# A decoder trunk's feed-forwards as one stream of seven-product blocks, with the down projection and with GpSimd making sums

## The chip, the cores and the metric

The kernel runs on one core of a Trainium2 chip. The metric is the device time of one launch in microseconds. The core's engines are named as in the profile: PE (matrix products), DVE (VectorE), ACT (ScalarE), POOL (GpSimd) and SP (SyncE, which issues the DMAs). They run side by side, each through its own instructions in their order, and wait for one another by semaphores.

## The reference

Two decoder layers run over 520 tokens: 512 of a new sequence and 8 single ones that continue older sequences. Each layer is a feed-forward, a mixer (latent attention in the first, a short convolution in the second) and another feed-forward. Cut to what matters here:

```python
D_MODEL = 1024
D_FF = 2816

def rmsnorm(x, g):
    xf = x.astype(jnp.float32)
    inv = lax.rsqrt(jnp.mean(xf * xf, axis=-1, keepdims=True) + EPS)
    return (xf * inv).astype(x.dtype) * g

def swiglu(h, wg, wu, wd):
    return (jax.nn.silu(h @ wg) * (h @ wu)) @ wd

    for i in range(DEPTH):
        xp = xp + 0.5 * swiglu(rmsnorm(xp, norm_ffn1[i]), w_ffn1_gate[i], w_ffn1_up[i], w_ffn1_down[i])
        ...
        xp = xp + mp
        xs = xs + ms
        xp = xp + 0.5 * swiglu(rmsnorm(xp, norm_ffn2[i]), w_ffn2_gate[i], w_ffn2_up[i], w_ffn2_down[i])
```

All is float32, and there are four feed-forwards, each with 1024 x 2816 weights for gate and up and 2816 x 1024 for down.

## The kernel before

The residual stream `xT` lies transposed in SBUF: 8 tiles of 128 features by 520 tokens, the tokens in two halves of 260. Every product of two float32 matrices is made of three matmuls: ACT rounds an operand to the "hi" part, DVE subtracts it from the operand and gets the "lo" part, and PE adds hi x hi, hi x lo and lo x hi in PSUM. So every weight passes through ACT (`split_hi`, `first_hi`, `up_hi`, ...) and DVE (`split_lo`, `first_lo`, ...), and so does every activation.

A feed-forward has 22 tiles of 128 hidden features, in two chunks of 11 (`CHUNK`). A tile needs the gate and the up product of all 8 feature tiles. The string `KINDS` says how: "C" is a plain tile (`plain_tile`, 2 x 8 x 3 matmuls for each half of the tokens, 96), "S" a block of seven products in place of eight (`block_tile`), in the manner of Strassen and Winograd: gate and up are the two columns, the two halves of the features the inner dimension, the two halves of the tokens the rows. Each product is `half_product` with 4 x 3 matmuls, 84 in all. Four of the seven use sums of weights, which POOL makes in `weight_sums` (four instructions of 512 elements a tile), and sums of token halves, which DVE and ACT make once for a feed-forward (`mix_diff`, `mix_base`, `mix_sums`, `mix_round`, `mix_rest`). Of the 22 tiles 13 are blocks; the first tile of each chunk is plain too and comes through `split_hi` and `split_lo`. The seven products of a block go into seven PSUM banks; DVE adds them up afterwards (`gate_first`, `gate_second`, `up_base`, `up_both`), multiplies by `inv` (the token's norm), ACT takes the silu, and DVE makes `hid_t`, which is rounded into `g_hi` and `g_lo`.

The split parts of the weights lie in a ring of six halves (`RING`), four in `w_hi`/`w_lo` and two in `x_hi`/`x_lo`; a part may be split as soon as PE has used the part six before it (`part_used`). The down projection of a chunk is plain: 8 output tiles x 11 x 3 x 2 = 528 matmuls, from units that go through `w_hi` alone; DVE scales each output tile and adds it to `xT`. In the second chunk's down projection the next stage's normalised input is made tile by tile (`publish_act`, `publish_dve`). SP loads each weight tile (512 KB) into one of the four slots of `raw` when the slot is free. PE does nothing but matmuls; its order is that of the code: two units, the tiles of the chunk, the down projection. At a stage's start `norm_pe` sums the squares, and `norm_dve` and `norm_act` make `inv`, with a reciprocal on DVE.

## Time and profile before

| | |
|---|---|
| median of three runs | 2437.41 us (2435.6 to 2437.86) |
| span of the profiled execution | 2426.2 us |
| PE busy | 2371.8 us, 98% |
| DVE busy | 1543.2 us, 64% |
| ACT busy | 987.8 us, 41% |
| POOL busy | 344.5 us, 14% |

The profile is one execution. Its span goes from the first to the last instruction on the core; the time of a run is some 11 us longer than that. Busy time counts an engine's instructions from start to end, overlapping ones once. Matmuls are pipelined: one of 260 columns has a duration of some 283 ns, but starts follow one another faster, so that a stretch is best read by its number of matmuls and its length. "PEclk" is the clock granted to PE, as a share of the full 2.4 GHz.

### The profile page before, as it was taken

To read this page: it belongs to the slowest core of one execution; us is meant where nothing else is said; L and a number is where in the kernel's file an instruction comes from. 1 tells how busy PE (TensorE), PEld (TensorE's weight loads), DVE (VectorE), ACT (ScalarE), POOL (GpSimd) and SP (SyncE) were. 2 spreads that over 40 slices of the span, in tenths; PEclk is the share of its full clock that TensorE was granted. 3 is DMA by queue.
4 is the path that set the end of the run, shared out by engine and by line. 5 is a ranking of instruction groups with operands and counts; after the bars stand their busy time and mean duration, and the time that the engine had idled before them with its cause. 6 is when DMAs were issued, how large, how long until landed. Compare 5 with 4: busy or idle time off the path is not lost.

```text
span 2426.2 us, 47136 instructions
## 1 busy us (share of the span) xinstructions
PE 2371.8 (98%) x18561; PEld 2307.0 (95%) x18561; DVE 1543.2 (64%) x2361; ACT 987.8 (41%) x1926; POOL 344.5 (14%) x226
## 2 busy tenths in 40 slices
PE   7999999999999999999999999999999999999998
PEld 7999999875999999989999999999999999999998
DVE  7855865555555555547865767864765666874773
ACT  5422433464455555534432434432433224432431
POOL 1412410000000000000312410312310000331320
PEclk9999999999999999999999999999999999999999
DMA  4324324210211111203323323323333332323332
GB/s 125 104 82 118 88 85 126 90 37 26 62 34 50 47 46 44 62 10 87 97 89 111 94 84 102 96 83 109 98 88 104 88 90 87 94 85 115 89 88 79
DMA packets 373257, 199.76 MB, mean 82 GB/s; under 512 B 31680, under 2 KB 369686, under 8 KB 373064
## 3 DMA queue, kind: packets, MB, share of 16 engines
q1 hardware_dynamic: 372884, 197.03, 28.1%
q8 instruction: 126, 2.06, 0.4%
q14 instruction: 67, 0.55, 0.1%
q10 hardware_dynamic: 180, 0.11, 0.0%
HBM read 194.27 MB, written 2.87 MB: 81 GB/s over the span
## 4 chain that ended last, share of the span: by engine, by line
PE 89%; DVE 6%; issue 2%; ACT 2%; DMA 0%; SPq 0%; ACTq 0%; DVEq 0%; POOL 0%; POOLq 0%
PE ps L1960 16%; PE ps L412 15%; PE ps L416 14%; PE ps L414 14%; PE ps L733 7%; PE ps L734 7%; PE ps L735 7%; PE ps L1886 1%; PE ps L1749 1%; PE ps L1774 1%; PE ps L1898 1%; ACT sq L2244 1%; PE ps L1889 1%; PE ps L1773 1%; DVE mix_lo L680 0%
## 5 line engine op out<-in xcount | busy, mean ns | idle before, releaser
L401 DVE TENSOR_TENSOR w_lo<-raw,w_hi 128x512 fp32r<-128x512 f32 (+2 forms) x200 | 202.9, 1014 | 346.1 <-ACT w_hi L395 341.0
L395 ACT CAST w_hi<-raw 128x512 fp32r<-128x512 f32 (+2 forms) x200 | 174.0, 870 | 466.7 <-PE ps L416 413.1
L412 PE MATMUL ps<-g_hi,w_hi 128*128 128x260 f32 x1408 | 284.5, 284 | 0.3
L416 PE MATMUL ps<-g_hi,w_lo 128*128 128x260 f32 x1408 | 283.7, 283 | 0.0
L414 PE MATMUL ps<-g_lo,w_hi 128*128 128x260 f32 x1408 | 283.4, 283 | 0.0
L629 POOL TENSOR_TENSOR wsum<-raw 128x512 f32<-128x512 f32 x52 | 73.4, 1411 | 1206.2 <-DMA raw<-in_w_ffn_up 869.3
L412 PE MATMUL ps<-h_hi,w_hi 128*128 128x260 f32 x1168 | 236.9, 284 | 5.1 <-DVE h_lo L2596 2.2
L416 PE MATMUL ps<-h_hi,w_lo 128*128 128x260 f32 x1168 | 235.5, 283 | 0.0
L414 PE MATMUL ps<-h_lo,w_hi 128*128 128x260 f32 x1168 | 235.4, 283 | 0.0
L2007 ACT ACTIVATE ksq<-ps 128x384 f32<-128x384 f32 (+1 forms) x384 | 146.8, 456 | 196.6 <-PE ps L1960 196.6
L412 PEld LDWEIGHTS ps<-g_hi,w_hi 128*128 128x128 f32 x1408 | 216.9, 188 | 1.1 <-issue 1.1
L414 PEld LDWEIGHTS ps<-g_lo,w_hi 128*128 128x128 f32 x1408 | 217.5, 188 | 0.0
L416 PEld LDWEIGHTS ps<-g_hi,w_lo 128*128 128x128 f32 x1408 | 217.2, 188 | 0.0
L412 PEld LDWEIGHTS ps<-h_hi,w_hi 128*128 128x128 f32 x1168 | 180.4, 189 | 6.3 <-DVE h_lo L2596 2.4
L416 PEld LDWEIGHTS ps<-h_hi,w_lo 128*128 128x128 f32 x1168 | 180.7, 189 | 0.0
L414 PEld LDWEIGHTS ps<-h_lo,w_hi 128*128 128x128 f32 x1168 | 180.5, 189 | 0.0
L1960 PE MATMUL ps<-wuk_hi,latT_hi 128*128 128x384 f32 (+2 forms) x768 | 173.7, 334 | 6.3 <-DVE latT_lo L2078 2.9
L1960 PE MATMUL ps<-wuk_lo,latT_hi 128*128 128x384 f32 (+1 forms) x768 | 173.5, 334 | 0.0
L1960 PE MATMUL ps<-wuk_hi,latT_lo 128*128 128x384 f32 (+1 forms) x768 | 162.2, 319 | 0.0
L882 ACT ACTIVATE silu_t<-gate_t 128x520 f32<-128x520 f32 x88 | 56.4, 641 | 254.5 <-DVE gate_t L1041 164.9
L2086 DVE TENSOR_REDUCE kss<-ksq 128x8 f32<-128x1024 f32 x128 | 154.7, 1209 | 0.0
L733 PE MATMUL ps<-mix_hi,w_hi 128*128 128x260 f32 x520 | 148.3, 285 | 0.8 <-DVE w_lo L606 0.8
(416 smaller groups left out, 5989.1 us busy)
## 6 DMA issues: line engine op xcount, KB each, us to landing
raw<-in_w_ffn_gate SPq DMA_DIRECT2D x88, 512.0 KB, 3.9
raw<-in_w_ffn_up SPq DMA_DIRECT2D x88, 512.0 KB, 4.4
raw<-in_w_ffn_down SPq DMA_DIRECT2D x64, 448.0 KB, 3.8
raw<-in_w_ffn_down SPq DMA_DIRECT2D x64, 256.0 KB, 2.7
cache<-in_cache_latent SPq DMA_DIRECT2D x128, 128.0 KB, 2.0
raw<-in_w_conv_in SPq DMA_DIRECT2D x24, 512.0 KB, 3.8
raw<-in_w_o_attn SPq DMA_DIRECT2D x8, 512.0 KB, 4.2
cache<-in_cache_krope SPq DMA_DIRECT2D x128, 32.0 KB, 1.8
```

Of the source, the lines that this page charges most:

```text
L395: nc.scalar.copy(w_hi[:, un.half, 0:n] if dst is None else dst, src).then_inc(unit_hi_made, 1)
L401: nc.vector.tensor_tensor(w_lo[:, un.half, 0:n], src, w_hi[:, un.half, 0:n], ALU.subtract).then_inc(unit_lo_made, 1)
L412: nc.tensor.matmul(o[b], hi, mh[:, x0 + b * HALF:x0 + (b + 1) * HALF], start=start, stop=False)
L414: nc.tensor.matmul(o[b], hi, ml[:, x0 + b * HALF:x0 + (b + 1) * HALF], start=False, stop=False)
L416: mm = nc.tensor.matmul(o[b], lo, mh[:, x0 + b * HALF:x0 + (b + 1) * HALF], start=False, stop=stop)
L629: nc.gpsimd.tensor_tensor(wsum5[:, 0, :], u1, u2, ALU.add).then_inc(sums_made, 1)
L733: nc.tensor.matmul(o, hi[:, kc], mh(k), start=k == 0, stop=False)
L734: nc.tensor.matmul(o, hi[:, kc], ml(k), start=False, stop=False)
L735: mm = nc.tensor.matmul(o, lo[:, kc], mh(k), start=False, stop=k == KH - 1)
L1960: mm = nc.tensor.matmul(ps[:, o + e, 0:nn], x, wd[:, c, c0:c0 + nn], start=(c == 0 and q == 0), stop=(c == KC - 1 and q == 2))
L2007: ins = nc.scalar.activation(ksq[:, t % 2, c0:c0 + nn], ps[:, o + e, 0:nn], ACT.Square)
L2086: nc.vector.tensor_reduce(kss[:, s, t, :], ksq[:, t % 2, :].rearrange("p (h d) -> p h d", h=H), AX.X, ALU.add).then_inc(kss_made, 1)
```

## The change

A feed-forward has no chunks any more. Its work is a list `ORDER` of 34 entries: the first tile (T), two plain ones (C), then 19 gate-and-up blocks (S) and 12 blocks of the down projection (D), which stand in three groups of four between the S. A D block takes two output tiles as the two columns, a group's pairs of hidden tiles (4, 4 and 3 pairs, `PAIRS`) as the inner dimension, and the token halves as the rows: seven products of 12 (or 9) matmuls. All blocks, S and D, share one code on each engine (`block`). So 31 blocks follow one another, each with four weight sums on POOL. The order of the seven products is new: m1, m2, m6, m3, m7, m5, m4, and three of them go on in the bank of m1, so that PSUM adds them; ACT copies the bank out in between (`keep_first`, `keep_second`, `keep_third`), and PE waits for the copy (`kept`) before it goes on in it.

For the down blocks the hidden tiles are needed as seven pieces of 260 columns: three raw and four sums. After each odd tile POOL makes the sums of the pair (`pair_mix`, one instruction of 520 elements and two of 260), ACT rounds all seven pieces (`pair_hi`, 1820 elements) and DVE subtracts (`pair_lo`, 1820). For the last pair, which the next block needs at once, both go in two parts. At the start of a feed-forward the normalised input gets the same seven pieces, for each of four pairs of feature tiles: DVE scales by gain and `inv` (`scaled_dve`), POOL mixes (`mix_pool`), ACT and DVE split (`set_hi`, `set_lo`). POOL also adds the down blocks' results to `xT` (`first_add`, `second_add`) and squares to `acc` for the next norm (`square_add`). The blocks' results need no product with `inv`. The core of the diff, its new side (the PE, ACT and DVE versions of `block` in this order; that of ACT ends with `silu` for an S block):

```diff
+        ORDER = ([("T", 0, 0), ("C", 0, 1), ("C", 0, 2)] + [("S", 0, y) for y in range(3, 8)] + [("S", 1, 0)]
+                 + [("D", 0, y) for y in range(4)] + [("S", 1, y) for y in range(1, 8)] + [("S", 2, 0)]
+                 + [("D", 1, y) for y in range(4)] + [("S", 2, y) for y in range(1, 6)] + [("D", 2, y) for y in range(4)])
+        SIZE = {"T": 0, "C": 6, "S": 8, "D": 8}
+        GATE, UP = 0, 2
+        M12, M63, M75, M4 = 0, 2, 4, 6
+        RING = 6
...
+        def weight_sums(pool, bk):
+            u1, u2, g1, g2 = bk.raw_half(1, 0), bk.raw_half(1, 1), bk.raw_half(0, 0), bk.raw_half(0, 1)
+            w = bk.width
+            s6, s3, s7, s5 = wsum63[:, 0:w], wsum63[:, w:2 * w], wsum75[:, 0:w], wsum75[:, w:2 * w]
+            ahead = blocks[bk.at][bk.b - 1] if bk.b > 3 else blocks[bk.at - 1][-1] if bk.at else None
             for j in (1, 0):
...
+                bk.loaded(pool, j)
             if ahead:
...
+                pool.wait_ge(part_lo_made, ahead.end(M75, 2))
+            nc.gpsimd.tensor_tensor(s5, u1, u2, ALU.add).then_inc(sums_made, 1)
+            pool.wait_ge(sums_made, 4 * bk.s + 1)
+            nc.gpsimd.tensor_tensor(s6, s5, g1, ALU.add).then_inc(sums_made, 1)
+            pool.wait_ge(sums_made, 4 * bk.s + 2)
+            nc.gpsimd.tensor_tensor(s3, s6, g2, ALU.add).then_inc(sums_made, 1)
+            nc.gpsimd.tensor_tensor(s7, u2, s6, ALU.subtract).then_inc(sums_made, 1)
...
+        def scaled_dve(dve, at, k):
+            bk = blocks[at][0]
+            f = scaled(at)[:, k % 2]
             if k >= 2:
...
+                dve.wait_ge(set_made, own_sets(at, k - 1))
+            for o, y in ((EA, k), (OA, k + KH)):
+                g = KD * GAIN[bk.stage] + y
+                ins = nc.vector.scalar_tensor_tensor(out=f[:, o * HALF:(o + 2) * HALF], in0=xT[:, y * T:(y + 1) * T],
+                                                     scalar=gain[:, g:g + 1], in1=inv[:], op0=ALU.mult, op1=ALU.mult)
+            ins.then_inc(scaled_made, 1)
...
+        def first_mix(tensor_tensor, f):
+            ea = f[:, EA * HALF:EB * HALF].unsqueeze(1).to_broadcast([P, 2, HALF])
+            return tensor_tensor(two(f[:, M0 * HALF:M1 * HALF]), ea, two(f[:, EB * HALF:OB * HALF]), ALU.subtract)
...
+        def pair_mix(pool, bk):
+            pool.wait_ge(hid_made, bk.t + 1)
+            pairs_read(pool, bk)
+            first_mix(nc.gpsimd.tensor_tensor, mixes[:]).then_inc(pair_mixed, 1)
+            pool.wait_ge(pair_mixed, 3 * bk.pair + 1)
+            nc.gpsimd.tensor_tensor(piece(M1), piece(M0), piece(OA), ALU.subtract).then_inc(pair_mixed, 1)
+            pool.wait_ge(pair_mixed, 3 * bk.pair + 2)
+            nc.gpsimd.tensor_tensor(piece(M3), piece(M1), piece(OB), ALU.add).then_inc(pair_mixed, 1)
...
+            nc.scalar.copy(pair_at(bk.at, bk.pair)[0][:, c0:c1], mixes[:, HALF + c0:HALF + c1]).then_inc(set_hi_made, n)
...
+            nc.vector.tensor_tensor(lo[:, c0:c1], mixes[:, HALF + c0:HALF + c1], hi[:, c0:c1], ALU.subtract).then_inc(set_made, n)
...
+                nc.gpsimd.tensor_tensor(xT[:, x0:x0 + T], xT[:, x0:x0 + T], gate_t[:], ALU.add).then_inc(first_added, 1)
...
+            for bk in blocks[at][3:]:
+                old = blocks[at][bk.b - 1]
+                if old.kind == "S" and old.odd:
+                    pair_mix(pool, old)
+                if bk.b + 1 < BLOCKS:
+                    weight_sums(pool, blocks[at][bk.b + 1])
+                elif more:
+                    for k in range(2, 6):
+                        square_add(pool, nc.gpsimd.tensor_tensor, n + 1, k)
+                if bk.out:
+                    first_add(bk)
+                    if bk.c < 2:
+                        second_add(bk)
+                    elif more and bk.d in (1, 2):
+                        square_add(pool, nc.gpsimd.tensor_tensor, n + 1, bk.d - 1)
...
+            def block(bk):
+                pe.wait_ge(part_lo_made, bk.end(M12, 2))
+                banks_free(bk)
+                rest, late = range(bk.pairs), range(0)
+                if bk.last_pair:
+                    rest, late = range(bk.pairs - 1, bk.pairs), range(bk.pairs - 1)
+                    pe.wait_ge(set_made, pair_sets(at, PAIRS_ALL * (at + 1) - 1))
+                    half_product(bk, M12, A, EB, True, False, late)
+                    half_product(bk, M12 + 1, B, OB, True, False, late)
+                    pe.wait_ge(part_lo_made, bk.end(M63, 2))
+                    half_product(bk, M63 + 1, C, OA, True, False, late)
+                    pe.wait_ge(set_made, pair_sets(at, PAIRS_ALL * (at + 1)) - 1)
+                elif bk.out and bk.d == 0:
+                    pe.wait_ge(set_made, pair_sets(at, PAIRS_ALL * at + sum(PAIRS[:bk.c + 1])))
+                half_product(bk, M12, A, EB, not late, True, rest).then_inc(part_used, 1)
+                half_product(bk, M12 + 1, B, OB, not late, True, rest).then_inc(part_used, 1)
+                pe.wait_ge(part_lo_made, bk.end(M63, 2))
+                pe.wait_ge(kept, 3 * bk.s + 1)
+                if bk.last_pair:
+                    half_product(bk, M63, A, M1, False, False, late)
+                    pe.wait_ge(set_made, pair_sets(at, PAIRS_ALL * (at + 1)))
+                half_product(bk, M63, A, M1, False, True, rest).then_inc(part_used, 1)
+                half_product(bk, M63 + 1, C, OA, not late, True, rest).then_inc(part_used, 1)
+                pe.wait_ge(part_lo_made, bk.end(M75, 2))
+                pe.wait_ge(kept, 3 * bk.s + 2)
+                half_product(bk, M75, A, M2, False, True).then_inc(part_used, 1)
+                half_product(bk, M75 + 1, E, M0, True, True).then_inc(part_used, 1)
+                pe.wait_ge(part_lo_made, bk.done)
+                pe.wait_ge(kept, 3 * bk.s + 3)
+                half_product(bk, M4, A, M3, False, True).then_inc(part_used, 2)
...
+            def keep_second(bk):
+                act.wait_ge(part_used, bk.end(M63))
+                nc.scalar.copy(gate_t[:, 0:HALF], ps[:, bk.bank, 0:HALF]).then_inc(kept, 1)
...
+            def block(bk):
+                old, nxt = own[bk.b - 1], own[bk.b + 1] if bk.b + 1 < BLOCKS else None
+                shown = more and bk.out and bk.c == 2 and bk.d > 0
+                k = 2 * bk.d - 2 if bk.out else 0
+                if bk.last_pair:
+                    pair_hi(act, old, RAW_PART)
+                m75_hi(act, bk)
+                if bk.last_pair:
+                    pair_hi(act, old, MIX_PART)
+                keep_first(bk)
+                m4_hi(act, bk)
+                if old.kind == "S" and old.odd and not bk.last_pair:
+                    pair_hi(act, old)
+                if shown:
+                    publish_hi(act, n + 1, k)
+                keep_second(bk)
+                if shown:
+                    square_act(act, n + 1, k)
+                if nxt:
+                    first_hi(act, nxt)
                 else:
...
+                    next_unit(0)
+                keep_third(bk)
+                if shown:
+                    publish_hi(act, n + 1, k + 1)
+                if nxt:
+                    m63_hi(act, nxt)
                 else:
...
+            def block(bk):
+                old, nxt = own[bk.b - 1], own[bk.b + 1] if bk.b + 1 < BLOCKS else None
+                shown = more and bk.out and bk.c == 2 and bk.d > 0
+                k = 2 * bk.d - 2 if bk.out else 0
+                pair = old.kind == "S" and old.odd
+                after(old)
+                if bk.last_pair:
+                    pair_lo(dve, old, RAW_PART)
+                    pair_lo(dve, old, MIX_PART)
+                m75_lo(dve, bk)
+                second_made(bk)
+                m4_lo(dve, bk)
+                if pair and not bk.last_pair:
+                    pair_lo(dve, old)
+                if shown:
+                    publish_lo(dve, n + 1, k)
+                first_begun(bk)
+                if nxt:
+                    first_lo(dve, nxt)
+                elif Unit(u0 + 2).n < LAST_UNIT:
+                    split_lo(dve, Unit(u0 + 2))
+                first_made(bk)
+                up_made(bk)
+                if nxt:
+                    m63_lo(dve, nxt)
+                elif Unit(u0 + 3).n < LAST_UNIT:
+                    split_lo(dve, Unit(u0 + 3))
+                if shown:
+                    publish_lo(dve, n + 1, k + 1)
```

What that makes of the orders, at three places. First POOL in the first feed-forward. Before, its last preparation and its first sums (`wsum5` and `wsum63` are the weight sums, `raw` the loaded weights):

```order
L2514 AFFINE_SELECT own<-own 8x64
L629 TENSOR_TENSOR wsum5<-raw 128x512
L633 TENSOR_TENSOR wsum63<-wsum5,raw 128x512
L635 TENSOR_TENSOR wsum63<-wsum63,raw 128x512
L638 TENSOR_TENSOR wsum5<-raw 128x512
```

After, in the block that follows an odd tile (`mixes` holds the pair's pieces, `wsum75` and `wsum63` the weight sums of the next block):

```order
L728 TENSOR_TENSOR mixes<-mixes 128x520
L772 TENSOR_TENSOR mixes<-mixes 128x260
L774 TENSOR_TENSOR mixes<-mixes 128x260
L705 TENSOR_TENSOR wsum75<-raw 128x512
L707 TENSOR_TENSOR wsum63<-wsum75,raw 128x512
L709 TENSOR_TENSOR wsum63<-wsum63,raw 128x512
L710 TENSOR_TENSOR wsum75<-raw,wsum63 128x512
```

Ahead of the four sums of the next block now stand the three sums of the pair, and they wait for the odd tile's `hid`.

Second, ACT around a block in the first feed-forward, before (L593, L602 and L612 are the block's weight sums, L564 and L574 the next tile's weights, L891 the copy of m1's bank, L882 silu, L886 the rounding of `hid_t`):

```order
L593 CAST w_hi<-wsum5 128x512
L602 CAST w_hi<-wsum63 128x1024
L886 CAST g_hi<-hid_t 128x520
L891 COPY up_t<-ps 128x260
L612 CAST x_hi<-wsum5 128x512
L564 CAST w_hi<-raw 128x1024
L574 CAST w_hi<-raw 128x1024
L882 ACTIVATE silu_t<-gate_t 128x520
```

After, from the m7 and m5 weight sums of the block that follows an odd tile (L677) to the next block's m6 and m3 (L667), and its silu:

```order
L677 CAST w_hi<-wsum75 128x1024
L999 COPY gate_t<-ps 128x260
L688 ACTIVATE x_hi<-raw 128x512
L782 CAST pairs1<-mixes 128x1820
L1003 COPY gate_t<-ps 128x260
L647 CAST w_hi<-raw 128x1024
L1016 COPY mixes<-ps 128x260
L667 CAST w_hi<-wsum63 128x1024
L990 ACTIVATE sq<-gate_t 128x520
```

The rounding of the pair's 1820 elements stands between the first and the second copy of the bank.

Third, DVE at the start of the first feed-forward, from the reciprocal, before:

```order
L470 RECIPROCAL sq<-inv 128x520
L997 TENSOR_TENSOR gate_t<-ps,inv 128x520
L668 TENSOR_TENSOR mix_f<-mix_f 128x260
L669 SCALAR_TENSOR_TENSOR mix_f<-xT,gain,mix_f 128x260
L671 SCALAR_TENSOR_TENSOR mix_f<-xT,gain,mix_f 128x260
L1013 TENSOR_TENSOR hid_t<-ps,silu_t 128x520
L668 TENSOR_TENSOR mix_f<-mix_f 128x260
L669 SCALAR_TENSOR_TENSOR mix_f<-xT,gain,mix_f 128x260
L671 SCALAR_TENSOR_TENSOR mix_f<-xT,gain,mix_f 128x260
L1017 TENSOR_TENSOR g_lo<-hid_t,g_hi 128x520
L680 TENSOR_TENSOR mix_lo<-mix_f,mix_hi 128x4x260
```

After (`scaled2` is the scaled input, `hs` its split pieces):

```order
L604 RECIPROCAL sq<-inv 128x520
L1100 TENSOR_TENSOR gate_t<-ps,inv 128x520
L721 SCALAR_TENSOR_TENSOR scaled2<-xT,gain,inv 128x520 x2
L1109 SCALAR_TENSOR_TENSOR mixes<-ps,inv 128x520
L1113 TENSOR_TENSOR mixes<-mixes,sq 128x520
L721 SCALAR_TENSOR_TENSOR scaled2<-xT,gain,inv 128x520 x2
L1100 TENSOR_TENSOR gate_t<-ps,inv 128x520
L651 TENSOR_TENSOR x_lo<-raw,x_hi 128x1024
L747 TENSOR_TENSOR hs<-scaled2,hs 128x1820
L721 SCALAR_TENSOR_TENSOR scaled2<-xT,gain,inv 128x520 x2
L747 TENSOR_TENSOR hs<-scaled2,hs 128x1820
L721 SCALAR_TENSOR_TENSOR scaled2<-xT,gain,inv 128x520 x2
```

Where single sums of 260 elements were made on DVE, there are now scalings of 520 (two at a time) and low parts of 1820, and the sums between them are POOL's.

## Rows read from the trace of the kernel before

**Rows 1.** The page, part 1 (PE) and part 4 (engines).

```profile
PE 2371.8 (98%) x18561; PEld 2307.0 (95%) x18561; DVE 1543.2 (64%) x2361; ACT 987.8 (41%) x1926; POOL 344.5 (14%) x226
...
PE 89%; DVE 6%; issue 2%; ACT 2%; DMA 0%; SPq 0%; ACTq 0%; DVEq 0%; POOL 0%; POOLq 0%
```

**Rows 2.** Busy time by stretch; the four stretches are the four feed-forwards.

```profile
core 0: us, PE busy (x) PEld busy (x) DVE busy (x) ACT busy (x) POOL busy (x), PEclk, DMA share, GB/s
12.00:389.20 377.20, 369.33 (x3033) 367.84 (x3034) 262.12 (x346) 147.87 (x218) 83.80 (x52) 0.99 0.34 96
1122.80:1488.50 365.70, 364.38 (x3020) 363.03 (x3019) 255.61 (x329) 140.16 (x203) 85.20 (x52) 1.00 0.33 94
1488.50:1854.20 365.70, 363.99 (x3018) 362.68 (x3017) 255.47 (x330) 140.08 (x203) 85.21 (x52) 1.00 0.33 96
2042.30:2413.70 371.40, 367.10 (x3028) 365.92 (x3027) 245.53 (x316) 130.46 (x188) 85.74 (x52) 0.99 0.30 87
```

**Rows 3.** The same view of one down projection of 528 matmuls.

```profile
145.20:208.80 63.60, 63.57 (x528) 63.57 (x529) 26.74 (x35) 14.00 (x18) 1.62 (x2) 1.00 0.37 106
```

**Rows 4.** The timeline, DVE and POOL: start us, us, engine, line, operation.

```profile
280.89 1.23 DVE L568 TENSOR_TENSOR w_lo<-raw,w_hi 128x1024 fp32r<-128x1024 f32 x1 [0.68 <-ACT w_hi L564]
281.10 2.18 POOL L635 TENSOR_TENSOR wsum<-wsum,raw 128x512 f32<-128x512 f32 x1
283.23 1.31 POOL L638 TENSOR_TENSOR wsum<-raw 128x512 f32<-128x512 f32 x1
283.48 1.61 DVE L1041 TENSOR_TENSOR gate_t<-gate_t,inv 128x520 f32<-128x520 f32 x1
```

**Rows 5.** Single lines: durations of one in ns, least, median and most.

```profile
L1041 DVE TENSOR_TENSOR gate_t<-gate_t,inv x52: 687/1602/1800, 71.0 to 2349.9; 128x520 f32<-128x520 f32 x52
L606 DVE TENSOR_TENSOR w_lo<-wsum,w_hi x36: 1217/2298/2309, 64.4 to 2344.2; 128x1024 fp32r<-128x1024 f32 x36
L635 POOL TENSOR_TENSOR wsum<-wsum,raw x52: 1282/2168/2301, 39.3 to 2337.3; 128x512 f32<-128x512 f32 x52
L1037 DVE TENSOR_TENSOR gate_t<-ps,gate_t x52: 427/428/430, 70.5 to 2348.9; 128x260 f32<-128x260 f32 x52
```

**Rows 6.** Groups by line and shape, ACT: busy us, mean ns, idle before.

```profile
L564 ACT CAST w_hi<-raw 128x1024 fp32r<-128x1024 f32 x52 | 54.5, 1048 | 54.4 <-PE ps L735 54.4
L584 ACT CAST w_hi<-raw 128x512 fp32r<-128x512 f32 x36 | 22.3, 618 | 23.0 <-PE ps L416 15.0 <-PE ps L735 8.0
L891 ACT COPY up_t<-ps 128x260 f32<-128x260 f32 x52 | 19.0, 366 | 0.0
L426 ACT ACTIVATE h_hi<-xT,gain 128x520 fp32r<-128x520 f32 x24 | 17.5, 731 | 61.9 <-DVE xT L1167 61.9
L433 ACT ACTIVATE sq<-xT 128x520 f32<-128x520 f32 x24 | 14.9, 622 | 0.0
```

**Rows 7.** Busy time by stretch: waits of PE and what follows them.

```profile
17.60:19.80 2.20, 0.07 (x1) 0.00 (x0) 1.88 (x3) 0.29 (x1) 0.00 (x0) 1.00 0.29 71
19.80:24.40 4.60, 4.53 (x25) 4.54 (x26) 4.32 (x8) 3.79 (x8) 0.00 (x0) 0.63 0.40 118
36.40:42.00 5.60, 4.15 (x35) 3.97 (x34) 4.83 (x6) 0.98 (x3) 5.30 (x4) 1.00 0.33 97
49.80:60.00 10.20, 6.15 (x39) 6.17 (x39) 10.02 (x16) 6.55 (x10) 0.00 (x0) 0.83 0.18 52
```

**Rows 8.** The timeline of DVE at the start of the third feed-forward.

```profile
1497.83 3.40 DVE L470 RECIPROCAL sq<-inv 128x520 f32<-128x520 f32 x1
1502.23 0.69 DVE L997 TENSOR_TENSOR gate_t<-ps,inv 128x520 f32<-128x520 f32 x1
```

**Rows 9.** Groups by line and shape, DVE; L437 reads two SBUF operands.

```profile
L437 DVE SCALAR_TENSOR_TENSOR h_lo<-xT,gain,h_hi 128x520 fp32r<-128x520 f32 x24 | 18.2, 760 | 20.6 <-ACT h_hi L426 20.6
```

**Rows 10.** PE's waits: engine, line, what for; us in total, times, longest.

```profile
PE ps L412 <- DVE x_lo L578: 9.2, 4, 4.2
```

**Rows 11.** The page, part 6: DMA issues of gate weights, median us to landing.

```profile
raw<-in_w_ffn_gate SPq DMA_DIRECT2D x88, 512.0 KB, 3.9
```

1170 lines of the change are left out of this document (536 added, 634 removed).

## The prediction

> **What bounds the kernel now.** First the busy times and the chain of work that ended last [rows 1]: PE is busy for 98% of the span and 89% of the chain is PE; nothing else has more than 6%. Then the stretches of the four feed-forwards [rows 2]: 377.2, 365.7, 365.7 and 371.4 us, PE busy in all but 1.3 to 8 of each. There DVE is busy for some 255 us, ACT for 140, POOL for 85. Then what a product costs: in one down projection 528 matmuls of 260 columns take 63.6 us at the full clock [rows 3], so 0.1205 us each, one after the other without a gap. So a matmul less in a feed-forward is worth 0.12 us, as long as the other engines deliver.
>
> **What leaves PE.** A tile of gate and up costs 96 matmuls plain and 84 as a block of seven products (7 x 4 x 3). Before, a feed-forward has 9 plain tiles and 13 blocks, 1956 matmuls, and a plain down projection of 1056: 3012. After: 3 plain tiles (288), 19 blocks (1596), and a down projection in 8 blocks of 84 and 4 of 63 (924): 2808. That is 204 less, 24.6 us for each feed-forward [rows 3], 98.3 us in all. A block of 84 lasts 10.1 us, one product of 12 matmuls 1.44 us.
>
> **What comes to DVE and POOL, and their common resource.** The trace shows that the two don't run side by side. [rows 4]: POOL's third sum starts at 281.10 while a DVE subtraction of two SBUF operands runs until 282.12; it takes 2.18 us instead of 1.28 and ends 1.16 us after DVE. DVE's product gate_t x inv starts at 283.48, POOL's fourth sum runs until 284.54, DVE ends at 285.09, 0.55 later. [rows 5] say it for all: gate_t x inv takes 0.69 us at best and 1.60 in the median, the 1024-wide subtraction L606 1.22 and 2.30, POOL's L635 1.28 and 2.17; L1037, which reads PSUM and one SBUF tile, is 0.43 at all times. So a DVE instruction with two SBUF operands and a POOL sum exclude each other. I charge what they add when one has waited: POOL 1.16 for 512 elements (1.17 for 520; for 260, which no row shows, between a half of it, 0.58, and all of it; I take 0.60, the half with a little of a start), DVE 1.08 for 1024 (1.23 less the 0.14 by which 0.69 exceeds 0.55), 0.56 for 520 and so on by size: 0.54, 0.29 and 1.90 for 512, 260 and 1820.
>
> Charge per block of 84. Weight sums 4 x 1.16 = 4.64; three 1024-wide low parts 3.24; the low part of m4 0.54; the first half of hid 0.29: 8.7 us. Every second gate/up block also has the pair's work: pair_mix 1.17 + 2 x 0.60 and pair_lo of 1820 elements 1.90, 4.3 us. Two such blocks: 21.7 us of exclusive work in 20.2 us of PE. A down block: 4.64 + 3.24 + 0.54 + first_add 1.17 + second_add 0.60 = 10.2 for 10.1. A down block of the last four: 4 x 0.87 + 2.43 + 0.41 + 0.29 + 1.17 = 7.8 for 7.58, and 10.1 where publish_lo (2 x 0.56) and a square_add (1.17) join. Before, POOL sums for 13 of 22 tiles only, and a run of plain tiles or down tiles in which POOL is idle follows each one or two blocks; now it sums for 31 blocks in a row.
>
> Here a page weighs in. The Trainium skill, "SBUF — State Buffer", section "Who interferes with whom", says that the pair of ports which VectorE and GpSimd share is an exclusive lock held for the whole instruction, and that two SBUF inputs on VectorE suffice against a GpSimd instruction that reads SBUF. The trace agrees that they exclude each other, but the second ends 1.16 us after the first, not 1.28. By whole durations two gate/up blocks would need 24.8 us instead of 21.7; what that makes of the time is the second rival.
>
> **The even gate/up block, worked out.** Time 0 is PE's start of the block after an odd one. In the block before, the slots for m6 and m3 come free after six products, at -1.44; ACT rounds 1024 elements (1.05 [rows 6]), DVE subtracts (1.22 [rows 5]) until +0.9, and hid takes two instructions of 0.4: done at 1.65. DVE's m75_lo goes first, until 2.75; POOL's first sum of the pair until 3.9; DVE's m4_lo until 4.5; POOL's other two until 5.8. ACT rounds the 1820 elements: from 0.62 for 512 and 1.05 for 1024 [rows 6] 1.74, until 7.6. Only then comes its keep_second (0.37), at 8.0, since pair_hi stands ahead of it in ACT's queue, and PE can't put m7 onto the bank before. It wanted to at 5.77: it waits 2.3 us. [rows 7] show what follows such a wait: after 2.2 us without a matmul (17.6 to 19.8) the granted clock of the next 4.6 us is 0.63 in the mean, and the stretch with the 4.05 us wait for x_lo (49.8 to 60.0) has 0.83, while the stretch with a wait of 1.45 us (36.4 to 42.0, for the gains) stays at 1.00. Both falls are 3.4 us at the lower level of 1.2 GHz (4.6 x 0.37 / 0.5, 10.2 x 0.17 / 0.5), so one costs 1.7 us. The even block thus takes 10.1 + 2.3 + 1.7 = 14.1 us; the odd block next to it finds the port free enough and takes 10.1. First_lo of the next block, due at 14.1, is done at 12.5. Without the clock's fall it would be 12.6 us, and +2.5. There are 9 such blocks in a feed-forward (after the odd tiles 3, 5, 7 of the first group, 1, 3, 5, 7 of the second, 1 and 3 of the third), 36 in all: 36 x 4.0 = **+144 us**, between 36 x 1.5 (nothing but the excess of 21.7 over 20.2) = 54 and 36 x 5.6 = 202 (the second rival).
>
> **The last pair** is needed at once by the first of the last down blocks. PE does two of three pieces in 2.2 us, waits for hid, pair_hi and pair_lo of 780 elements (about 4.4), and then for all sums, since keep_first stands behind the second pair_hi: about 12.1 instead of 7.6 us, and a fall of the clock. +5.5 each, 4 times **+22** (12 to 36).
>
> **The start of a feed-forward.** Before, inv is there 13.4 us after the start of a later one (reciprocal of 3.40 us, then gate_t at 1502.2, start 1488.5 [rows 8]). From there DVE has now, up to up_lo of the second plain tile: the gate, four times two scaled instructions (0.56 each where charged, 0.76 alone [rows 9]), hid, first_lo, two set_lo of 1.90; POOL has three mixes of 2.4 and four sums of 1.16 between them, and each waits for the other. Added in the order of the queues, up_lo is done at 37; PE wants it at 29.6 (unit 5.8, norm 0.6, unit 5.8, tile 11.6, half a tile 5.8) and waits 7.5 us. The rest (two more set_lo, hid, first_lo, the last mix, pair_mix, pair_hi, pair_lo, and only then m63_lo) ends at 52.4, where block 3 wants it at 44.6 + 2.9: 4.9 more. With one fall of the clock not covered, m6 of block 3 comes 15.5 us later than without waits. Between 10 and 22. Before has losses there too, which go: the x_lo waits are 9.2 us in all [rows 10], 4.05 of it in [rows 7] and a like one in the last feed-forward, with the clock behind them 16 us. Net 62 - 16 = **+46**.
>
> **Smaller.** The last down group with the publishing: three blocks with 10.1 against 7.58, slack of about 2.5: +5, in three feed-forwards, +15. At the stage boundary POOL's four square_adds stand ahead of the last first_add, on which x_ready waits: h_lo of tiles 6 and 7 comes some 1.5 us late, 3 times, +4.5. ACT's work there is two publish_hi, two squares, three copies and four parts of 768 and 384 elements, 1.46 + 1.24 + 1.1 + 3.0 = 6.8 us in 7.6 [rows 6]: nothing by itself. The weights are the same bytes, and a load may start when the block before last has given its slot back, well ahead of the 4 us from issue to landing [rows 11]: nothing, and if that cover went, POOL would wait on raw. The attention and convolution stages are unchanged.
>
> **Sum.** -98.3 + 144 + 22 + 46 + 15 + 4.5 = +133 us. On the profiled execution's 2426.2 us of span that is 2559; the median lies 11.2 above that span, and gets the same 11.2: 2437.4 + 133 = **2571 us**.
>
> **Rivals.** (1) The exclusion is absorbed, and it is faster. If POOL's sums fall where DVE waits or reads PSUM, only the bare chain of the pair is left: hid at 1.65, three sums in 2.75, rounding 1.74, keep_second, 6.65 against 5.77, 0.9 us x 36 = 32, the last pairs 14, the start 2 each against the 16 that go. 2437 - 98 + 32 + 14 + 8 - 16 = 2377. For it: DVE's five PSUM instructions in a block give POOL 2.1 us. Against: 21.7 us of exclusive work in 20.2 can't be hidden by any order. It decides at an exclusive load under 20 us for two blocks. (2) Whole durations are charged: 24.8 us for two blocks, hid comes later each round, the even block waits for 4.9 us and first_lo for 0.65: 25.8 for two, +5.6 instead of 4.0, 2571 + 58 = 2629. (3) The waits are as I say, but the clock doesn't fall after 2.3 us, which is close to the 2.2 seen: 2571 - 36 x 1.5 = 2517. (4) The exclusive work is packed without a gap and nothing else is late: the low ends of all terms, 2437 - 98 + 54 + 12 + 24 + 9 + 3 = 2441, no change. For it: the rings and halves let DVE work some 3 us ahead. Against: keep_second's place behind pair_hi, which no packing moves.
>
> **How the numbers follow.** Chances: my sum 0.48, rival 2 0.20, rival 3 0.18, rival 1 0.10, rival 4 0.04. The range goes from 2475 (rival 3 less the low ends of start and last pair, 22 + 10, and half of the 20 under Smaller) to 2650 (rival 2 and most of the start's high end); it leaves out rivals 1 and 4. A measurement of this kernel can tell about 0.2%, 5 us. Faster 0.11, same 0.02, slower 0.87.
>
> **What would show it.** Right: PE busy well under 98%, with waits of the m7 products on ACT's gate_t copy (keep_second) 36 times 2 to 3 us; POOL's 512-element sums at 2 us and more in the mean and DVE's 1024-wide low parts from wsum and raw well over 1.22; a granted clock under 0.95 in the feed-forwards; feed-forwards of about 400 us each, down blocks near 10.2 us. Wrong: sums at 1.3 us beside DVE's subtractions, even blocks of 10 to 11 us (then rival 1), or waits that PE has for wsum's low parts instead of the bank (then the port's load and not the order of ACT's queue sets the time).

## The result, and the profile after

The change makes the kernel slower: 2613.22 us in the median of four runs (2604.61 to 2622.16) against 2436.51 (2430.78 to 2437.86) for the kernel before in the same job, a ratio of 1.0728 with a 95% interval of 1.0695 to 1.0761. The prediction was 2571 us with a range of 2475 to 2650, so the direction and the range held, and the number was 42 us short. The profiled execution took 2604.61 us and has a span of 2602.8. A run's time is thus 1.8 us longer than its span, as in all runs below; the 11 us named for the kernel before lie between the span of one execution and the median of others. The four executions differ by their clock: the mean granted clock is 0.964 and 0.960 in the two of 2604.61 and 2606.72 us, 0.957 and 0.953 in those of 2619.72 and 2622.16.

The page of the kernel after, part 1 and the engines of part 4, which answer to [rows 1]:

```profile
PE 2357.2 (91%) x17745; PEld 2270.8 (87%) x17745; DVE 1808.2 (69%) x2462; ACT 1231.8 (47%) x2234; POOL 1260.3 (48%) x792
...
PE 53%; POOL 23%; issue 10%; DVE 7%; ACT 5%; DMA 0%; POOLq 0%; SPq 0%; ACTq 0%; DVEq 0%
```

816 matmul records fewer, as the prediction counts them, and yet PE's busy time is only 14.6 us less, for the most part because more of the matmuls run at the lower level of the clock: by the mean granted clock (0.992 before, 0.964 after) some 39 us of the span before and 187 us after are at 1.2 GHz. POOL, which had no share of the chain to speak of, now has 23% of it. The four feed-forwards in the view of busy time by stretch, which answer to [rows 2]:

```profile
core 0: us, PE busy (x) PEld busy (x) DVE busy (x) ACT busy (x) POOL busy (x), PEclk, DMA share, GB/s
12.80:434.10 421.30, 366.64 (x2829) 359.79 (x2829) 328.27 (x364) 208.22 (x293) 312.42 (x193) 0.94 0.30 85
1170.60:1577.60 407.00, 361.17 (x2814) 355.14 (x2812) 313.95 (x347) 200.32 (x278) 313.21 (x193) 0.95 0.29 84
1579.00:1994.20 415.20, 360.28 (x2812) 353.43 (x2813) 324.61 (x357) 201.14 (x280) 316.54 (x195) 0.95 0.29 84
2183.90:2590.50 406.60, 361.03 (x2822) 354.87 (x2820) 307.68 (x346) 191.44 (x265) 304.51 (x189) 0.95 0.27 80
```

Together 1650.1 us against 1480.0 before: 170 of the 176.6 us by which the span grew. POOL's busy time went from 85 us to over 300 in each, DVE's from some 255 to some 320.

What PE waits for (engine, line, releaser; us in total, times, longest):

```profile
PE ps L936 <- ACT gate_t L1003: 97.6, 39, 3.0
PE ps L532 <- DVE w_lo L661: 25.2, 4, 6.6
PE ps L936 <- ACT gate_t L999: 20.7, 34, 1.9
PE ps L936 <- DVE w_lo L671: 18.8, 5, 4.5
PE ps L532 <- DVE x_lo L651: 9.0, 3, 6.7
PE ps L936 <- ACT mixes L1016: 6.0, 1, 6.0
```

L1003 is keep_second, the copy of the bank onto which m7 is added. It is the wait that the prediction put first, in 36 even blocks and a few others. L661 is the low part of the third tile's up weights, L671 that of the sums for m6 and m3, L651 of a raw weight, L999 and L1016 the first and third copy of a block.

An even block is a gate-and-up block behind an odd tile, in which a pair is finished. The timeline of one, whose first matmul is at 227.76, from the moment hid is done (start us, us, engine, line, operation, idle before and releaser):

```profile
229.67 0.41 DVE L1144 SCALAR_TENSOR_TENSOR mixes<-ps,sq 128x260 f32<-128x260 f32 x1
230.00 1.21 DVE L681 TENSOR_TENSOR x_lo<-wsum,x_hi 128x1024 fp32r<-128x1024 f32 x1
230.16 2.23 POOL L728 TENSOR_TENSOR mixes<-mixes 128x520 f32<-128x520 f32 x1 [1.84 <-DVE mixes L1144]
...
233.63 0.73 POOL L774 TENSOR_TENSOR mixes<-mixes 128x260 f32<-128x260 f32 x1
...
234.44 1.71 ACT L782 CAST pairs<-mixes 128x1820 fp32r<-128x1820 f32 x1 [2.87 <-POOL mixes L774]
...
236.06 0.37 ACT L1003 COPY gate_t<-ps 128x260 f32<-128x260 f32 x1
236.25 2.58 DVE L788 TENSOR_TENSOR pairs<-mixes,pairs 128x1820 fp32r<-128x1820 f32 x1 [3.31 <-ACT pairs L782]
...
236.57 0.36 PE L936 MATMUL ps<-hs,x_hi 128*128 128x260 f32 x1 [2.90 <-ACT gate_t L1003]
```

It reads as a relay. hid ends 2.3 us into the block; POOL's first sum waits behind DVE's L681 and lasts 2.23 us for about 1.3 of work; the last sum ends at 6.6, the cast at 8.4, keep_second at 8.7, and PE, which wanted that copy at 5.8, has stood still for 2.9 us. Another even block and the same one, by stretch:

```profile
89.20:103.51 14.31, 11.82 (x86) 11.64 (x85) 9.89 (x11) 6.83 (x10) 11.76 (x7) 0.88 0.25 74
...
227.76:241.12 13.36, 10.46 (x86) 10.09 (x84) 9.92 (x11) 6.81 (x9) 11.21 (x8) 1.00 0.27 80
```

In the first the granted clock fell, 3.4 us at 1.2 GHz (14.31 x 0.12 / 0.5); in the second it stayed at 2.4 GHz. Of the 36 such blocks the clock fell in 25, in one of them for 6.8 us; they take 14.4 us in the mean, the 11 others 13.3.

### The profile page after: what moved, and what is told of

Same layout as the page of the kernel before. It is cut to its first block, busy times and chain, and to the rows that moved or that the text cites. A ratio compares the mean times of both kernels' runs of the same rounds, so it can differ in the third digit from the quotient of the medians.

```text
span 2602.8 us, 47588 instructions
## 1 busy us (share of the span) xinstructions
PE 2357.2 (91%) x17745; PEld 2270.8 (87%) x17745; DVE 1808.2 (69%) x2462; ACT 1231.8 (47%) x2234; POOL 1260.3 (48%) x792
## 3 DMA queue, kind: packets, MB, share of 16 engines
HBM read 194.27 MB, written 2.87 MB: 76 GB/s over the span
## 4 chain that ended last, share of the span: by engine, by line
PE 53%; POOL 23%; issue 10%; DVE 7%; ACT 5%; DMA 0%; POOLq 0%; SPq 0%; ACTq 0%; DVEq 0%
PE ps L2024 15%; PE ps L936 7%; PE ps L938 7%; PE ps L937 7%; POOL mixes L728 4%; PE ps L532 3%; PE ps L536 3%; PE ps L534 3%; POOL xT L828 3%; POOL wsum L710 3%; POOL wsum L705 2%; POOL wsum L709 2%; POOL wsum L707 2%; POOL mixes L772 2%; POOL mixes L774 1%
## 5 line engine op out<-in xcount | busy, mean ns | idle before, releaser
L936 PE MATMUL ps<-hs,w_hi 128*128 128x260 f32 x1512 | 449.1, 297 | 84.3 <-ACT gate_t L1003 63.8
L937 PE MATMUL ps<-hs,w_hi 128*128 128x260 f32 x1512 | 444.0, 294 | 0.0
L938 PE MATMUL ps<-hs,w_lo 128*128 128x260 f32 x1512 | 443.5, 293 | 0.0
L936 PEld LDWEIGHTS ps<-hs,w_hi 128*128 128x128 f32 x1512 | 302.4, 200 | 92.6 <-issue 72.1
L937 PEld LDWEIGHTS ps<-hs,w_hi 128*128 128x128 f32 x1512 | 303.3, 201 | 0.0
L938 PEld LDWEIGHTS ps<-hs,w_lo 128*128 128x128 f32 x1512 | 302.3, 200 | 0.0
L710 POOL TENSOR_TENSOR wsum<-raw,wsum 128x512 f32<-128x512 f32 (+1 forms) x124 | 272.7, 2199 | 0.0
L705 POOL TENSOR_TENSOR wsum<-raw 128x512 f32<-128x512 f32 (+1 forms) x124 | 173.0, 1395 | 190.6 <-DVE w_lo L681 144.7
L936 PE MATMUL ps<-hs,x_hi 128*128 128x260 f32 x728 | 213.4, 293 | 42.6 <-ACT gate_t L1003 32.0
L709 POOL TENSOR_TENSOR wsum<-wsum,raw 128x512 f32<-128x512 f32 (+1 forms) x124 | 223.3, 1801 | 9.7
L936 PE MATMUL ps<-pairs,w_hi 128*128 128x260 f32 x720 | 207.9, 289 | 21.1 <-ACT gate_t L999 13.2
L937 PE MATMUL ps<-hs,x_hi 128*128 128x260 f32 x728 | 211.2, 290 | 0.0
L938 PE MATMUL ps<-hs,x_lo 128*128 128x260 f32 x728 | 210.9, 290 | 0.0
L937 PE MATMUL ps<-pairs,w_hi 128*128 128x260 f32 x720 | 204.4, 284 | 0.0
L938 PE MATMUL ps<-pairs,w_lo 128*128 128x260 f32 x720 | 204.1, 283 | 0.0
L532 PE MATMUL ps<-h_hi,w_hi 128*128 128x260 f32 x800 | 166.9, 290 | 33.2 <-DVE w_lo L661 25.2
L936 PEld LDWEIGHTS ps<-hs,x_hi 128*128 128x128 f32 x728 | 142.8, 196 | 47.1 <-issue 34.1
L651 DVE TENSOR_TENSOR w_lo<-raw,w_hi 128x1024 fp32r<-128x1024 f32 (+1 forms) x80 | 150.5, 1881 | 42.0 <-ACT w_hi L647 41.9
```

The costliest lines, as they stand in the source:

```text
L532: nc.tensor.matmul(o[b], hi, mh[:, x0 + b * HALF:x0 + (b + 1) * HALF], start=start, stop=False)
L651: nc.vector.tensor_tensor(ring(LO, bk, M12, 2), bk.raw_row(0), ring(HI, bk, M12, 2), ALU.subtract).then_inc(part_lo_made, 2)
L705: nc.gpsimd.tensor_tensor(s5, u1, u2, ALU.add).then_inc(sums_made, 1)
L709: nc.gpsimd.tensor_tensor(s3, s6, g2, ALU.add).then_inc(sums_made, 1)
L710: nc.gpsimd.tensor_tensor(s7, u2, s6, ALU.subtract).then_inc(sums_made, 1)
L936: nc.tensor.matmul(o, hi[:, kc], mh[:, xc], start=start and k == 0, stop=False, skip_group_check=goes_on)
```

## The experiments

Each ratio is to runs of the kernel before on the same chip, which took 2429.14 us in the median beside small_sums, copy_first, dve_pair_sums and new_order and 2436 to 2437 us beside the others. The intervals are of 95%. The blocks of each kernel can be told by PE's records, since each has 84 (or 63) matmuls of 260 columns. This table, worked out from them, gives for each kind of block how much longer it was than its matmuls at 0.1203 us, summed over the four feed-forwards, us. An odd block is any other of gate and up but block 3, the first of a feed-forward. The even row depends on how often the clock fell in that execution: in 25 of the 36 in the kernel after, 32 in small_sums, 26 in copy_first, 8 in free_third and none in dve_pair_sums, new_order, both_cuts and filler.

```
blocks          after small_sums copy_first dve_pair_sums new_order free_third both_cuts filler
block 3 (4)      32.4    32.5      30.6        32.6         30.5      30.6       32.6     31.1
even (36)       142.8   143.1     129.3        83.3         13.5      71.6        3.5    118.0
odd (36)          4.5    -1.2      29.4         6.3        133.9      93.0       -1.2      6.3
down 1, 2 (32)    8.1    -0.9       7.6        13.8         22.0      27.5       -1.0     13.6
last pair (4)    22.4    22.5      22.7        11.3         23.8      26.0       14.9     25.0
last down (12)   30.3    18.6      29.9        33.5         29.2      30.7       20.0     28.6
```

### small_sums: the load of the port

POOL makes the weight sums of all blocks but the first of each feed-forward for 4 columns only, so this part of the computation is left out:

```diff
-            w = bk.width
+            w = bk.width if bk.s % BLOCKS_S == 0 else 4
```

> After the change, but of the weight sums on POOL only those of the first block of each feed-forward are made in full; those of the other 30 blocks are made for 4 columns only (the rest of the operand is stale), so this part of the computation is left out and its time on POOL and on the common port goes. Everything else is the same, the pair's sums on POOL too. Theory A (the even gate/up block waits because the pair's own chain, hid, three sums on POOL in turn with m75_lo and m4_lo, pair_hi, keep_second, is too long): the even blocks stay at 13 to 14.4 us (excess 3 to 4.2 us over 84 x 0.1203 = 10.1), only the small excesses of down blocks (0.5 each), of the last group (30 us in all) and half of the start's 68 go: 2613 - 10 - 20 - 25 = about 2555 us. Theory B (the summed load of the port, 21.7 us for two blocks, sets the pace): the load falls to 12.4 us and the even blocks to 11.0 us (0.9 of excess, the bare chain): about 2445 us.

Measured: 2586.92 us (2583.4 to 2590.43), ratio 1.0638 (1.0574 to 1.0702). PE's waits and three stretches of it, an odd block, the even one behind it, and a down block:

```profile
PE ps L936 <- ACT gate_t L1003: 92.5, 40, 2.5
...
218.80:228.88 10.08, 10.08 (x87) 10.08 (x86) 6.58 (x11) 5.37 (x9) 0.75 (x4) 1.00 0.25 72
228.88:243.14 14.26, 11.77 (x87) 11.59 (x86) 8.61 (x12) 6.85 (x10) 4.75 (x7) 0.88 0.34 98
300.18:310.28 10.10, 10.10 (x86) 10.10 (x85) 6.78 (x9) 4.92 (x7) 4.13 (x7) 1.00 0.36 103
```

POOL's busy time falls from 1260.3 to 555.9 us, DVE's in an odd block from 9.3 us to 6.6, and the even block takes 14.26 us as before. So most of the even block's wait isn't the summed load of the port. It is the length of the relay behind hid, in which only the sums of the pair itself stand. The load has a small share: PE's wait for keep_second is 2.5 us in all 36 blocks here. In the kernel after it is 2.5 us where the clock fell in the even block two blocks before, and 2.9 where it didn't. The 4 blocks without a fall take 12.8 us here, the 11 in the kernel after 13.3 in the mean. More falls (32 for 25) took that gain back. What the weight sums cost by holding DVE up are the 26 us of the other rows of the table: 12 in the last down group, 15 in odd and down blocks. The gain was half of what the first theory gave. It had the even blocks stay as they are, and they did (143.1 us for 142.8, with 108.8 us at the lower level instead of 88.4). What it had wrong is the start: none of the 25 us that it took off there went (block 3 has 32.5 us for 32.4, and the wait for the third tile's up weights 25.1 for 25.2), and 12 instead of 20 in the last down group.

The run's interval only touches that of the kernel after (1.0695 to 1.0761), so the 26 us rest on the table. In the profiled execution the attention stage, which the edit doesn't touch, took 746.6 us at a clock of 0.97 instead of 736.5 at 0.99 and hid 10 of them.

### copy_first: the place in ACT's queue

```diff
-                if old.kind == "S" and old.odd and not bk.last_pair:
-                    pair_hi(act, old)
                 if shown:
                     publish_hi(act, n + 1, k)
                 keep_second(bk)
+                if old.kind == "S" and old.odd and not bk.last_pair:
+                    pair_hi(act, old)
```

> After the change with one step of ACT moved: keep_second, the second copy of the bank, now stands ahead of pair_hi. All is computed. If its place in ACT's queue is the whole of the wait, the even block falls from 14.3 to 10.1 us, 36 x 4.0 = 143 us: 2470 us. By my timeline, the same work still has to pass: pair_lo until 10.1, POOL's third sum, then first_lo of the next block until 12.4 to 12.5 us after the start, and PE waits 2.3 us at the next block's start instead of 2.3 at m7, with the clock falling or not: even and odd block together 22.5 to 24.3 us instead of 24.3: between 2550 and 2613 us, and the wait moves to w_lo/x_lo of L651.

Measured: 2624.44 us (2623.07 to 2625.81), ratio 1.0792 (1.0736 to 1.0849): no gain over the kernel after. PE's wait for keep_second is down from 97.6 us to 1.7, and this stands in its place:

```profile
PE ps L936 <- ACT mixes L1016: 101.2, 37, 5.9
```

The wait was expected at the low parts of L651 if it moved; it moved to another place. L1016 is the third copy, which goes into the buffer mixes and so has to wait until pair_lo has read the pair out of it. The queue's order decides which copy is late; that one is late follows from the relay, which has to end inside the block.

### dve_pair_sums: a shorter relay

```diff
-                if old.kind == "S" and old.odd:
-                    pair_mix(pool, old)
 ...
                 after(old)
+                if pair:
+                    pair_mix(dve, old)
```

> After the change with the pair's three sums on DVE, straight after hid, in place of POOL (only the first pair's, at the start, stay on POOL). All is computed. Charged load for two blocks 20.5 us instead of 21.7, and the chain is hid 1.65, sums 3.3, pair_hi 5.1, keep_second 5.5, where PE wants it at 5.77. Theory A: the wait for keep_second goes nearly (0 to 0.4 us), what is late next is first_lo of the next block behind pair_lo, 1.5 us, without a fall of the clock: excess of the even block 1 to 2 us instead of 4.0, 2613 - 36 x 2.5 = about 2523 us. If POOL's sums were not what made it late, the time stays near 2613.

Measured: 2556.24 us (2556.01 to 2556.48), ratio 1.0512: 57 us less than the kernel after. An even block and the odd one behind it, and PE's waits:

```profile
222.61:235.09 12.48, 10.69 (x86) 10.15 (x84) 12.38 (x14) 6.82 (x9) 7.59 (x5) 1.00 0.30 86
235.09:245.30 10.21, 10.21 (x86) 10.21 (x86) 9.35 (x13) 5.57 (x9) 6.99 (x5) 1.00 0.36 104
...
PE ps L935 <- ACT mixes L1015: 58.6, 37, 5.8
PE ps L935 <- ACT gate_t L998: 17.3, 42, 1.0
PE ps L935 <- ACT gate_t L1002: 12.6, 39, 0.7
```

The three sums take DVE 1.5 us instead of POOL's 4.2. The even blocks take 12.4 us instead of 14.1, and in none of the 36 did the clock fall: the wait is cut into pieces of some 0.3 us (0.7 at most) and 1.5. DVE's busy time, the third column, shows the next bound: DVE works 12.38 of the 12.48 us.

### both_cuts: both at once

The edits of dve_pair_sums and of small_sums together, so the weight sums are left out here too.

> VectorE makes the three sums of each pair (as in dve_pair_sums) and GpSimd's weight sums are cut to 4 columns of each piece (as in small_sums, which leaves that part of the computation out). In dve_pair_sums VectorE was busy 12.38 of an even block's 12.48 us, 2.8 us of it the stretch that GpSimd's weight sums put on its operations. Theory A (what is left of the even blocks' wait there is VectorE's own full load, holds by the shared port included): with the holds gone the even blocks fall to 10.1 to 10.6 us, so the 83 us of the even blocks go nearly all, and about 30 us of the others: 2440 to 2460 us. Theory B (the wait is the queue place of the pair's two steps on ScalarE and VectorE, whatever they share a port with): the even blocks stay at 12.4 and only some 25 us go: 2520 to 2530 us.

Measured: 2436.33 us (2431.17 to 2443.78, eight runs), ratio 1.0012 (0.9992 to 1.0032): the same as the kernel before. An even block:

```profile
1312.26:1322.48 10.22, 10.22 (x86) 10.13 (x85) 9.65 (x15) 6.84 (x10) 2.79 (x4) 1.00 0.33 99
```

small_sums alone brought 26 us, dve_pair_sums alone 57, both 177 (22, 53 and 174 by the ratios). That they do more together says that the even block has two bounds, one behind the other: the relay through POOL, and when that is gone, DVE with the time that POOL's weight sums hold it. Take one away and the other still stands at 12.4 us or more; take both and the block is at its matmuls' 10.1. The starts, the last pair and the last down group are left, 68 us by the table, and with what the starts wait ahead of block 3 they use up the 98 us of the matmuls that went.

### new_order and free_third: a pair's steps put later

new_order puts pair_hi behind the block's third copy, pair_lo behind up_made, and lets an even block's third copy wait for the pair's sums alone (not shown):

```diff
                 keep_third(bk)
+                if old.kind == "S" and old.odd and not bk.last_pair:
+                    pair_hi(act, old)
 ...
                 up_made(bk)
+                if pair and not bk.last_pair:
+                    pair_lo(dve, old)
```

> After the change with the same instructions in another order: in the block after an odd tile ACT's pair_hi goes behind first_hi and keep_third, DVE's pair_lo behind first_lo, first_made and up_made, and keep_third of an even tile waits for the pair's sums instead of its low parts. All is computed. Theory A (order and latency of one chain): all that PE waits for in the even block, keep_second 4.7, first_lo 8.3, keep_third 7.6 us after its start, is in time, the excess falls from 4.0 to 0 to 0.5: 2613 - 36 x 3.7 = about 2480 us. Theory B (load of the port): two blocks still need 21.7 us of exclusive work against 20.2, excess at least 1.5 for each even block, 2613 - 36 x 2.5 = 2523 us or more.

Measured: 2630.64 us (2625.5 to 2635.78), ratio 1.0818 (1.0743 to 1.0892). The load theory gave 2523 us or more, the other one 2480. free_third goes further: the third copy has a buffer that is free by then, so nothing of the block waits for the pair, the roundings come last, and ACT's first copy goes ahead of the cast of the last sums:

```diff
-                nc.scalar.copy(bk.first(), ps[:, bk.bank, 0:HALF]).then_inc(kept, 1)
+                nc.scalar.copy(inv[:, 0:HALF], ps[:, bk.bank, 0:HALF]).then_inc(kept, 1)
 ...
-                m75_hi(act, bk)
                 if bk.last_pair:
+                    m75_hi(act, bk)
                     pair_hi(act, old, MIX_PART)
                 keep_first(bk)
+                if not bk.last_pair:
+                    m75_hi(act, bk)
```

> The third copy of a block no longer goes into the pair's buffer but into one that is free by then, so the pair has until the tile's hidden values are written, a block later, to be read out; its two roundings go behind the block's copies on ScalarE and VectorE, and ScalarE's first copy goes ahead of the cast of the last sums. GpSimd still makes the pair's sums. Theory A (even blocks wait since the pair's chain has to end inside the block): the third copy comes in time and the even blocks fall from about 14.1 to 10.1 to 11.5 us, odd ones grow by up to 1 us since the weight sums come late behind the pair's on GpSimd: 2490 to 2540 us. Theory B (GpSimd and VectorE together hold the shared port too much for 10.1 us a block): the wait comes back at another operation, 2590 us or more.

Measured: 2651.42 us (2648.43 to 2654.41), ratio 1.0877 (1.0845 to 1.0908), where the second theory gave 2590 or more. PE's waits, of new_order first and then of free_third:

```profile
PE ps L936 <- ACT gate_t L999: 105.0, 49, 3.6
PE ps L936 <- DVE w_lo L671: 24.1, 19, 4.5
```

```profile
PE ps L936 <- DVE w_lo L671: 61.3, 60, 4.5
PE ps L936 <- DVE pairs L788: 56.4, 8, 7.1
```

Both do what they were made for: the even blocks fall to 10.5 and 12.1 us in the mean. The odd ones rise from 10.2 to 13.8 and 12.7, and in free_third the first down block of each group waits up to 7.1 us for a pair that comes too late for it. In free_third's odd block the sums that it needs were begun behind the pair's on POOL:

```profile
239.16 0.75 POOL L774 TENSOR_TENSOR mixes<-mixes 128x260 f32<-128x260 f32 x1
239.87 2.29 POOL L705 TENSOR_TENSOR wsum<-raw 128x512 f32<-128x512 f32 x1
...
244.82 1.27 POOL L710 TENSOR_TENSOR wsum<-raw,wsum 128x512 f32<-128x512 f32 x1
```

An even block and an odd one together, by the table: 24.3 us in the kernel after, 24.6 in copy_first, 24.3 in new_order, 24.8 in free_third. With POOL making both kinds of sums, the orders that were tried moved the loss from one block or one copy to the other, and none made it smaller.

### filler: what the clock costs

18 matmuls more, whose result is overwritten, right ahead of the wait for keep_second:

```diff
                 pe.wait_ge(part_lo_made, bk.end(M75, 2))
+                before = blocks[at][bk.b - 1]
+                if before.kind == "S" and before.odd and not bk.last_pair:
+                    half_product(bk, M75 + 1, E, M0, True, False, range(2))
+                    half_product(bk, M75 + 1, E, M0, False, True)
                 pe.wait_ge(kept, 3 * bk.s + 2)
```

> The kernel after with 18 matmuls more, whose result is overwritten, in each of the 36 blocks that wait for the second copy, right ahead of that wait: 2.2 us of work in a wait of up to 3.1 us, 648 matmuls in all. Theory A (beside the wait itself, the fall of the granted clock behind it costs 1 us and more in most of these blocks, and comes from the engine standing idle): the clock stays at full in these blocks, they take 13.3 us instead of 14.1 on average, and the whole takes 2575 to 2595 us although it does more. Theory B (the clock falls whatever the engine does while its data are late, or the extra work delays the chain): no gain or a loss of up to 20 us: 2610 to 2635 us.

Measured: 2593.53 us (2590.29 to 2596.78), ratio 1.0644 (1.0609 to 1.0678). The kernel does 648 matmuls more, 78 us of PE's work, and is 20 us faster than the one after. The same block as above:

```profile
227.70:241.12 13.42, 12.73 (x105) 12.28 (x103) 9.98 (x11) 6.79 (x9) 11.27 (x8) 1.00 0.27 80
```

All 36 even blocks now take 13.4 us and none has a lower clock; they spend 25 us less (142.8 against 118.0 in the table). The relay's end didn't move, so this is the clock's share of these blocks: of the 4.0 us, 3.3 are the relay and the rest the falls of the clock.

The kernel after shows the price of one fall by itself. Among its blocks with a wait of 2.47 to 2.50 us, those with a fall take 14.1 to 14.3 us and the two without 12.93 and 12.94; among those with 2.81 to 2.87 it is 14.6 to 14.7 against 13.3. So a fall costs 1.3 us where it happens. Some 0.4 of it comes back: in the next even block, two blocks on, the wait is 2.5 us, and 2.9 where there was no fall. The means of 14.4 and 13.3 us mix the two and give 1.1.

### start_order and sums_late: the start

start_order puts the third tile's up weights ahead of the second set's low part on DVE, and what block 3 needs ahead of the first pair:

```diff
             scaled_dve(dve, at, 2)
+            up_lo(dve, own[2])
             set_lo(dve, at, 1)
             scaled_dve(dve, at, 3)
-            up_lo(dve, own[2])
 ...
-            pair_lo(dve, own[1])
             m63_lo(dve, own[3])
+            pair_lo(dve, own[1])
```

> Only the order at the start of each feed-forward differs: the low part of the third tile's up weights goes ahead of the second set's, and the cast, low part and SiLU that block 3 needs go ahead of the first pair's roundings. Theory A (the place in the queue costs): the wait for the up weights (25.2 us in four) goes and that for the sums' low part (18.8 in four) falls to 1.5 each: 2613 less 25 to 40, so 2573 to 2590 us. Theory B (the chain of the four sets' mixes on VectorE and GpSimd ends where it ends): the up wait only moves to the sets' own wait ahead of block 3, and at most 12 us go: 2600 to 2613 us.

Measured: 2624.38 us (2622.89 to 2625.87), ratio 1.0766 (1.0734 to 1.0797), not told apart from the kernel after. The second feed-forward's block 3 now waits at its first product for the low part of its own weights:

```profile
1226.76 0.59 PE L936 MATMUL ps<-hs,x_hi 128*128 128x260 f32 x1 [6.90 <-DVE x_lo L651]
```

So the up weights' wait moved, as the second theory had it. That the time lies above its 2600 to 2613 us goes in good part with the clock, which fell in 31 even blocks instead of 25: their excess is 159.2 us for 142.8. sums_late has the same edits and moves block 3's weight sums on POOL:

```diff
-            weight_sums(pool, blocks[at][3])
             mix_pool(pool, at, 2)
             mix_pool(pool, at, 3)
+            weight_sums(pool, blocks[at][3])
```

> start_order, and besides GpSimd makes block 3's weight sums behind the mixes of all four sets instead of between the second and the third. In the kernel after, those sums took 9.5 us of GpSimd in the second feed-forward's start (1193.5 to 1203.0) while the third set stood ready from 1198.8, and VectorE's operations beside them ran up to 3.4 us. Theory A (the start's extra wait is this chain: sets' mixes held by the sums): block 3 starts 4 to 7 us earlier in each feed-forward, and the sums are still in time for their product: 2573 to 2600 us. Theory B (VectorE's own work at the start is the bound): the start stays as long as it was and only other operations wait: 2610 to 2630 us.

Measured: 2616.45 us (2612.61 to 2620.3), ratio 1.0738 (1.0698 to 1.0777). PE in the second feed-forward's start, in the kernel after and then in sums_late:

```profile
1207.11 0.77 PE L532 MATMUL ps<-h_hi,w_hi 128*128 128x260 f32 x2 [6.55 <-DVE w_lo L661]
1217.15 0.39 PE L936 MATMUL ps<-hs,x_hi 128*128 128x260 f32 x1 [1.09 <-DVE hs L747]
1223.66 0.59 PE L936 MATMUL ps<-hs,w_hi 128*128 128x260 f32 x1 [4.45 <-DVE w_lo L671]
```

```profile
1215.38 0.58 PE L936 MATMUL ps<-hs,x_hi 128*128 128x260 f32 x1 [3.53 <-DVE x_lo L651]
1218.44 0.59 PE L936 MATMUL ps<-hs,x_hi 128*128 128x260 f32 x1 [0.74 <-DVE hs L747]
1229.00 0.56 PE L936 MATMUL ps<-hs,w_hi 128*128 128x260 f32 x1 [6.94 <-ACT gate_t L999]
```

The wait for the up weights, 6.55 us, is 0.68 in start_order and gone in sums_late. In sums_late block 3 starts 4.3 to 5.0 us earlier in the three later feed-forwards, as its first theory said, but lasts 5 us longer each (52.6 us over its matmuls instead of 32.4), now for its first copy, which ACT has behind the cast of the first pair, and POOL ends that pair's sums at 1225.8, 10.5 us into block 3 instead of 3.7: its queue is as long as before, block 3's weight sums stand right ahead of them and end at 1222.1, and block 3 itself starts earlier. The start is a chain over all four engines, and orders that were tried only choose where it shows.

### last_order: the last down group

```diff
-                if bk.b + 1 < BLOCKS:
+                ahead = bk.out and bk.c == 2
+                if ahead:
+                    first_add(bk)
+                if bk.b + 1 < BLOCKS:
```

and the convolution's first two weight loads are issued ahead of the wait for the last block.

> In the last group of down blocks GpSimd adds a block's first tile ahead of the next block's weight sums, and the first two weight loads of the convolution are issued ahead of the wait for the last feed-forward block. Theory A (the last group's 30 us over its matmuls are the add behind the weight sums and, once, 6.0 us behind the convolution's load): 8 to 18 us go, 2595 to 2605 us. Theory B (the sums then come late instead): only the 6 us of the load go, 2607 us.

Measured: 2688.25 us (2686.01 to 2690.49), ratio 1.1028, 75 us slower than the kernel after: neither theory. The load did what it should (the wait of 6.0 us for L1016 is gone). The other edit was a mistake about what first_add waits for. POOL in the last down blocks of the first feed-forward:

```profile
419.18 1.32 POOL L828 TENSOR_TENSOR xT<-xT,gate_t 128x520 f32<-128x520 f32 x1 [7.95 <-DVE gate_t L1135]
420.44 1.03 POOL L705 TENSOR_TENSOR wsum<-raw 128x384 f32<-128x384 f32 x1
```

The add needs the block's own m5, the sixth of its seven products, so POOL stands idle for 8 us with the next block's weight sums queued behind, in all 16 blocks of the last groups. Behind the last pair's each such block takes 13.3 to 14.4 us instead of 7.8 to 10.8 (one had 17.2, with the load), and the clock falls in all 12: the row of the last down group grows from 30.3 us to 77.5. The sums have to go first; the group's price isn't the order on POOL.

### combo: what may help, together

dve_pair_sums with the buffer of free_third, the start of sums_late and the convolution's load of last_order.

> What helped so far or may: VectorE makes the pairs' sums (dve_pair_sums), the third copy goes into a buffer that is free, so that it doesn't wait for the pair's low parts (from free_third, with the pair's steps where the kernel after has them), block 3's weight sums and its casts as in sums_late, and the convolution's first weights as in last_order. Theory A (each of these waits was its own): 2554 less about 30 for the even blocks' third copy, 20 for the starts and 6 for the load: 2490 to 2505 us, still slower than before. Theory B (VectorE, busy all of an even block in dve_pair_sums, only hands its lateness on to the next block): 2525 to 2545 us, the starts and the load alone.

Measured: 2554.64 us (2554.53 to 2554.75), ratio 1.0484 (1.0454 to 1.0514): no better than dve_pair_sums. Two blocks and a little more of it:

```profile
216.00:240.00 24.00, 22.01 (x182) 21.62 (x181) 23.05 (x27) 13.02 (x18) 14.86 (x9) 1.00 0.35 103
```

PE's longest waits are now for the first weights of the next block:

```profile
PE ps L935 <- DVE x_lo L651: 45.0, 23, 5.0
PE ps L935 <- DVE w_lo L651: 35.5, 23, 1.7
```

DVE is busy 96% of the time, and the even blocks take 12.5 us (12.4 in dve_pair_sums) although no copy waits for the pair any more: VectorE hands its lateness on, as in the second theory, whose 2525 to 2545 us it missed by 10. Block 3 starts 3 to 5 us earlier in each feed-forward and takes that back (51.3 us over its matmuls instead of 32.6). The last down group falls from 33.5 to 25.6 us, mostly by the load, and the even blocks and the last pair grow by 4. No version that was run and computes the whole beats the kernel before.

## Why the prediction was right, and where it was short

**The gain on PE** was 98.3 us, a count of matmuls times 0.1205 us, and nothing in the runs speaks against it: in small_sums and both_cuts odd and down blocks take their matmuls' time to 0.1 us.

**The exclusion** [rows 4, 5] holds in the new places with the sizes charged, where it strikes. L710, which adds 512 elements, has a median of 2.28 us; the 1024-wide L651 one of 1.97 into w_lo; L1121, which reads PSUM, stays at 0.41. pair_lo takes 2.59 in the median and 2.05 at least. But it doesn't strike everywhere: L705 and L707 have medians of 1.29 and 1.30 us, L651 into x_lo 1.52 and L681 1.22, so the sign named, sums of 2 us and more in the mean, did not come (1.76 over the four).

**The even block** was predicted as a relay of 4.0 us over the block, 144 us in all; measured 142.8. Its parts: hid at 2.3 us for 1.65, sums at 6.6 for 5.8, cast at 8.4 for 7.6, copy at 8.7 for 8.0, so PE waits 2.9 us there where I had 2.3 (2.7 in the mean of the 36). The clock fell in 25 of the 36 and not in all, and a fall cost 1.3 us where I had 1.7. By filler the block without any fall is 3.3 us over its matmuls, where I had 2.3, and the falls add 0.7, where I had 1.7. Both parts were off, in opposite directions, and that they cancel is luck; the order of events is as it was written. That the relay and not the summed load sets most of the time is shown by small_sums; that it comes back elsewhere when only the queue is changed, by copy_first. What I had not seen is that DVE's own busy time stands just behind it: dve_pair_sums ran straight into that bound, with DVE busy for 12.38 + 9.35 us of 12.48 + 10.21.

**The last pair**: 22 predicted, 22.4 measured.

**The start**: 62 us of new loss less 16 that would go, +46. The new waits are what was worked out: 6.3 us in the mean for the up weights (7.5 predicted), 0.8 to 1.7 for the sets and 4.5 for m6's low part (4.9 predicted together). The step that failed is the 16 us that should go with the x_lo waits [rows 10]. They did not go: 9.2 us before, 9.0 after. In the last feed-forward the wait shrank from 4.23 to 2.03 us, and in the first it grew from 4.05 to 6.67. I had said that before's losses vanish, without following the steps that bring x_lo there. By the rows themselves 16 us was too much: two of the four waits make 8.3 of the 9.2 us, and with a fall of 1.7 behind each of these two it is 12.6. What the feed-forwards grew by beyond the blocks of the table is 170 + 98 - 208 (240.5 over the matmuls, less the 32.4 of block 3) = 60 us: starts with block 3 and boundaries, where I had 46 + 4.5. That is 10 us of the miss.

**The last down group**: +15 predicted, 30.3 measured. I gave the blocks with publishing a slack of 2.5 us; the second and third of them are 3.2 and 2.6 us over without any. In the first feed-forward:

```profile
413.16:423.94 10.78, 8.30 (x63) 7.74 (x63) 10.78 (x13) 6.27 (x13) 8.96 (x7) 1.00 0.30 91
```

In that block, the second behind the last pair, DVE is busy for all of the 10.78 us. I had compared 10.1 us of exclusive work with 7.58 and left out DVE's work that excludes nobody, five instructions of 0.41 us in this block. In small_sums 12 of the 30 us go and this block falls from 10.8 to 8.7 us, but the group's last stays at 10.2 to 10.3; POOL has four squares to add in it and no weight sums. In filler 1.7 us go, in copy_first 0.4. Besides, once, 6.0 us: PE waited for the third copy of the last block ahead of the convolution, since ACT had the convolution's first cast in front of it, and the load for that cast was issued only after the block's weights were done. "Nothing by itself" was said of ACT's amount of work, and the load behind it wasn't looked at; last_order shows that issuing it earlier removes the wait.

**Down and odd blocks**: 0 predicted, 12.6 measured, about half a microsecond in the third and fourth block of each down group and in the block behind it, and nothing in the first two. The charge of 10.2 for 10.1 us stood in the prediction, and I took it for hidden. In small_sums and both_cuts the blocks have no excess at all, so it is POOL's weight sums beside DVE.

**The rivals.** The second, whole durations charged, gave 2629 us, and the measured 2613 lies between it and my sum. It isn't what happened: it wanted 25.8 us for two blocks, and they took 24.3 in the mean. The third, no fall of the clock, is settled by the records, and filler gives its size: 25 us over 36 blocks for it and 36 x 1.7 = 61 by my term. The first and the fourth, in which the exclusion or the load is absorbed, fell with the 97.6 us of PE's waits for keep_second.

**The miss in sum**: last down group 15, down and odd blocks 13, starts and boundaries 10, and 7 us of span outside the four feed-forwards (176.6 less 170), less 1 for the even blocks and 1 for the distance of median and span (10.4 us for 11.2): 43 of the 42.

**What stays open.** The 7 us outside the feed-forwards have no cause shown: 2.9 of them are in attention, 1.6 in the convolution, 1.4 between the second and the third feed-forward and 0.8 ahead of the first. The starts are known by a difference. Whether a start exists in which neither wait comes back was tried in two orders, not more. Why 11 of the 36 even blocks kept the clock and 25 lost it is not explained. The length of the wait alone doesn't decide it (it fell behind 17 of the 19 shortest waits and 8 of the 17 longest).

## What to carry to other kernels

A step that two engines pass back and forth inside the block that waits for it is priced by its length and not by its load. Write it down as a relay, from the event that starts it to the copy that PE needs, with each queue that it passes; moving one station in its queue moves the wait and not the end.

Before an algorithm that saves matmuls is paid for with sums on other engines, add up the busiest helper's full load for one block, holds by a shared port and PSUM reads included, and compare it with the block's new length. Here 12 of 96 matmuls less per tile, 1.44 us, was bought with a load of VectorE of 9.4 us in an odd block's 10.2.

A term that credits losses of the old kernel as gone needs its own working, as one that charges new losses does.

## What the runs showed of the hardware

Work with no use made the kernel faster: 18 matmuls in a wait of up to 3.0 us kept the granted clock at 2.4 GHz in 36 of 36 blocks, where 25 of them had lost it for 3.4 us (one for 6.8), and brought 20 us of 2613. Waits of some 0.3 us (0.7 at most) and 1.5 us in one block, with matmuls between them, never cost the clock in the 36 even blocks of dve_pair_sums.

A wait of the same length cost the clock in one block and not in another: it fell behind 17 of the 19 waits of 2.47 to 2.50 us and behind 8 of the 17 of 2.69 to 2.96. At like waits a block with a fall is 1.3 us longer (14.3 us against 12.9, and 14.7 against 13.3), less than the 1.7 that its 3.4 us at half the clock suggest.
